# Shared expert's products between the first expert blocks, and two orders mended, in a two-layer mixture-of-experts kernel

## The chip, the cores and the metric

The kernel runs on one core of a Trainium2 chip as one program of some 58,000 instructions. Its engines work side by side, each in its own order, and wait for one another through semaphores: TensorE (PE; its loading of weights is shown as PEld), VectorE (DVE), ScalarE (ACT), GpSimd (POOL) and SyncE (SP), which issues most DMAs. The metric is the time in microseconds (us) that the core takes for the whole program. Before the change it is 2652.32 us, the median of 3 runs (2647.43 to 2654.61).

## The reference, cut to what matters

Two layers of a diffusion backbone with 256 latent and 256 context tokens, D = 1024. Each layer is a mixer (layer 0: mLSTM and SSD heads, layer 1: latent attention and RWKV-7 heads) and then a mixture of experts. In layer 0 the experts see all 512 tokens, in layer 1 the 256 latent ones. All of it is float32.

```
def swiglu(x, wg, wu, wd):
    return (silu(x @ wg) * (x @ wu)) @ wd            # 1024 -> 512 -> 1024

def moe(v, router_w, router_bias, w_gate, w_up, w_down, s_gate, s_up, s_down):
    aff = sigmoid(xt @ router_w)                      # 16 experts in 4 groups
    ...                                               # the best group, in it the two best experts
    out = swiglu(xt, s_gate, s_up, s_down)            # the shared expert: every token
    for e in range(16):
        out = out + gates[:, e:e + 1] * swiglu(xt, w_gate[e], w_up[e], w_down[e])
```

The routed experts are computed only for the tokens that chose them. Which ones these are is known on the chip alone, once the router has run.

## The kernel before, in words

**An expert layer** is the function `moe_block`. TensorE computes the router's logits and turns the 512 (or 256) tokens from columns to rows; DVE finds for each token its two experts (`route_masks`), and, once TensorE has counted the tokens of each expert ahead of each token (`positions`), a row number in a list sorted by expert (`route_slots`). GpSimd writes each token's row twice into the list `x_sorted` in HBM (`rows_scattered`). The list is cut into blocks of 32 rows; each expert fills whole blocks, at least one. There are 47 blocks in layer 0 and 31 in layer 1 (`n_blocks`); those that the tokens leave over at the end count to the last expert. For each block, TensorE multiplies its 32 rows by the gate and up weights of its expert in two halves (`gate_up`, lines 1569 and 1570), turns the hidden values (`turn_hidden`, line 1578) and multiplies by the down weights (`down`, line 1591); for each pair of blocks the rows of x are turned first (`turn_x`, line 1554).

**Weights.** An expert has 2 MB of gate, 2 MB of up and 2 MB of down weights, 6 MB in all. There is room for three experts, three places: place 0 and 1 in the arena, place 2 in the ring that elsewhere holds the streamed weights of other products, and in which the shared expert's three pieces lie when the layer starts. The blocks are dealt to the places in contiguous parts: place p takes the blocks from `first_of[p]` on, and step i of the loop takes the next block of place `i % 3`. So in layer 0 place 0 has the blocks 0 to 15, place 1 16 to 31, place 2 32 to 46; in layer 1 0 to 10, 11 to 20, 21 to 30. A block's weights are loaded only if its expert differs from that of the block before it (`cond=new`; a table on the chip tells), and always for the first block of a place. SP issues these loads in the order of the steps, the first half of gate and up (lines 1440 and 1441) after the place's last block is done with its first half, the second half after its second, the down weights (line 1444) one step later. A load that is not wanted is issued too, but moves nothing.

**The shared expert** is computed between the router and the first block, in one go: 4 gate products and 4 up products of 8 matmuls each (`shared_rows`), then the down products of 4 matmuls each (8 in layer 0, 4 in layer 1; line 368 as all products through the helper `mms`). Only when they are done can the ring be loaded as place 2. The tokens' rows for the first blocks are read into `m_x`, which lies over the shared expert's input, and so not before its gate and up products are over.

**The mixer of layer 0** has the function `project_rest`: 32 products, of which ACT splits each weight into a high part (line 680), POOL makes the low part (line 690), TensorE multiplies and ACT reads out the result (lines 944 to 948). Meanwhile DVE makes the gates' running sums; ACT's exponentials for it (lines 936, 793, 795) stand ahead of the products' first split, in the order in which ACT works.

## Time and profile before

| what | value |
|---|---|
| median of 3 runs | 2652.32 us |
| the profiled execution's own time | 2651.06 us |
| its span, first to last instruction | 2649.3 us |
| PE busy, share of the span | 81% |
| DVE, ACT, POOL busy | 38%, 27%, 13% |
| router and shared expert of layer 0, from 853 us to the first block at 959.86 | 107 us |
| blocks of layer 0 | to 1321 us |
| router and shared expert of layer 1, from 2268 us to the first block at about 2324 | 56 us |
| blocks of layer 1 | to 2617 us |

The positions are those of the profiled execution, in us from its first instruction. A group of the profile is a line of the kernel with its operation and its tiles (what it writes, an arrow, what it reads). A busy TensorE is not one at its peak. A time in brackets behind a row is idle time of the engine before that instruction, and what ended it. "PEclk" is the clock granted to TensorE, 1.00 being 2.4 GHz and 0.50 being 1.2 GHz. "SPq" and "ACTq" are the issues of DMAs by these engines.

### The profile page before, as it was taken

What the parts mean: (1) busy time and instruction counts of PE and PEld (TensorE: products, weight loads), DVE (VectorE), ACT (ScalarE), POOL (GpSimd) and SP (SyncE); (2) the same over time, 40 slices, a digit from 0 to 9 for tenths busy, and PEclk for the clock granted to TensorE, in tenths of its full rate; (3) what the DMA queues carried; (4) which work ended last, traced back from release to release, by engine and by line L of the source; (5) the groups of instructions that cost most, each with busy time, mean ns of one, the idle gap of its engine ahead of it and who ended that gap; (6) DMA issues with size and microseconds to landing.
All of it is one profiled execution on the core that took longest, in us unless ns stands there. A gap on an engine that the chain in (4) does not pass through costs nothing. (4 is left out here: it accounts for less than half of the span.)

```text
span 2649.3 us, 57779 instructions
## 1 busy us (share of the span) xinstructions
PE 2141.1 (81%) x25731; PEld 1417.6 (54%) x25731; DVE 1010.6 (38%) x1602; ACT 706.4 (27%) x1499; POOL 350.6 (13%) x232
## 2 busy tenths in 40 slices
PE   5879999788796987797838869867887888877776
PEld 2457764343483544454523458557887866633333
DVE  0352506756504211111142257556576652311112
ACT  2222622255413000010020232354644420100001
POOL 0223320000142100000010024222131100000000
PEclk7989998778897999998968889979999988888788
DMA  7244540320324478987731012000000023599994
GB/s 246 98 169 155 187 162 1 116 75 0 96 95 167 185 255 308 316 276 266 275 140 69 0 56 88 0 3 4 4 4 4 4 74 119 174 376 341 344 337 162
DMA packets 180957, 381.00 MB, mean 144 GB/s; under 512 B 11242, under 2 KB 40518, under 8 KB 180454
## 3 DMA queue, kind: packets, MB, share of 16 engines
q1 hardware_dynamic: 163118, 344.02, 36.5%
q10 hardware_dynamic: 14136, 20.72, 2.6%
q0 software_dynamic: 3456, 12.58, 1.3%
q8 instruction: 202, 3.31, 0.5%
q14 instruction: 45, 0.37, 0.0%
HBM read 634.46 MB, written 25.95 MB: 249 GB/s over the span
## 5 line engine op out<-in xcount | busy, mean ns | idle before, releaser
L1569 PE MATMUL banks<-arena 128*32 128x256 f32 x1696 | 238.4, 430 | 105.6 <-DMA arena<-in_exp_w_up_dram 105.6
L368 PE MATMUL banks<-parts 128*128 128x512 f32 (+1 forms) x1096 | 241.0, 373 | 23.6 <-DVE parts L382 20.4
L1570 PE MATMUL banks<-arena 128*32 128x256 f32 x1696 | 238.4, 430 | 0.0
L368 PEld LDWEIGHTS banks<-parts 128*128 128x128 f32 x1096 | 194.3, 192 | 59.7 <-DVE parts L382 11.5
L1569 PEld LDWEIGHTS banks<-arena 128*32 128x32 f32 x1696 | 107.1, 121 | 196.8 <-DMA arena<-in_exp_w_up_dram 114.2
L376 DVE TENSOR_TENSOR arena<-banks,arena 64x256 f32<-64x256 f32 (+3 forms) x128 | 65.2, 511 | 334.0 <-ACT arena L1633 264.4
L2225 PE MATMUL banks<-arena 64*64 64x64 f32 x4224 | 155.7, 221 | 45.1 <-DVE arena L379 18.1
L1633 ACT ACTIVATE arena<-banks 64x256 f32<-64x256 f32 x78 | 29.7, 380 | 588.5 <-PE banks L1570 588.5
L368 PE MATMUL banks<-arena,ring 128*128 128x256 f32 (+2 forms) x544 | 161.7, 460 | 12.7 <-PEq L315 12.7
L2225 PEld LDWEIGHTS banks<-arena 64*64 64x64 f32 x4224 | 144.0, 136 | 51.0 <-DVE arena L379 19.4
L2225 PE MATMUL banks<-ring 64*64 64x64 f32 x4224 | 156.0, 220 | 11.8 <-issue 11.6
L368 PE MATMUL banks<-arena 128*64 128x128 f32 (+9 forms) x492 | 135.8, 430 | 36.8 <-PEq L315 25.0
L2225 PEld LDWEIGHTS banks<-ring 64*64 64x64 f32 x4224 | 143.3, 135 | 12.7 <-issue 12.2
L368 PE MATMUL banks<-h_parts,parts_z 128*128 128x512 f32 x416 | 133.9, 402 | 17.2 <-POOL parts_z L690 13.3
L368 PEld LDWEIGHTS banks<-arena,ring 128*128 128x128 f32 (+1 forms) x544 | 105.4, 195 | 67.1 <-issue 56.0
L368 PEld LDWEIGHTS banks<-arena 128*128 128x128 f32 (+5 forms) x492 | 74.3, 196 | 89.5 <-issue 60.5
L1591 PE MATMUL banks<-arena 128*32 128x256 f32 x1696 | 107.0, 395 | 17.0 <-DMA arena<-in_exp_w_down_dram 17.0
L1784 POOL DMA_INDIRECT arena<-y_sorted,slot_ids x12 | 11.3, 945 | 746.1 <-DMA y_sorted<-arena 743.1
L1569 PE MATMUL banks<-ring,arena 128*32 128x256 f32 x800 | 99.9, 393 | 8.9 <-DMA ring<-in_exp_w_up_dram 8.9
L1570 PEld LDWEIGHTS banks<-arena 128*32 128x32 f32 x1696 | 106.6, 121 | 0.0
L690 POOL TENSOR_TENSOR parts_z<-ring,parts_z 128x1024 fp32r<-128x1024 f32 x34 | 84.3, 2482 | 158.4 <-ACT parts_z L680 139.1
L1229 PE MATMUL banks<-arena 128*64 128x256 f32 (+3 forms) x288 | 89.8, 467 | 13.8 <-DVE arena L1262 13.8
(341 smaller groups left out, 3772.8 us busy)
## 6 DMA issues: line engine op xcount, KB each, us to landing
arena<-in_exp_w_gate_dram SPq DMA_DIRECT2D x106, 1024.0 KB
arena<-in_exp_w_up_dram SPq DMA_DIRECT2D x106, 1024.0 KB
arena<-in_exp_w_down_dram SPq DMA_DIRECT2D x53, 2048.0 KB
ring<-in_exp_w_gate_dram SPq DMA_DIRECT2D x50, 1024.0 KB
ring<-in_exp_w_up_dram SPq DMA_DIRECT2D x50, 1024.0 KB
ring<-in_exp_w_down_dram SPq DMA_DIRECT2D x25, 2048.0 KB
ring<-in_w_mod_dram SPq DMA_DIRECT2D x24, 2048.0 KB, 8.0
ring<-in_ab_w_in_dram SPq DMA_DIRECT2D x10, 2048.0 KB, 12.8
```

The source lines that it names most:

```text
L368: m = nc.tensor.matmul(o, a, b, start=first and n == 0, stop=last and n == len(pairs) - 1)
L376: return nc.vector.tensor_tensor(o, a, b, ALU.mult)
L690: nc.gpsimd.tensor_tensor(low, landed_part(j), whole(high), ALU.subtract).then_inc(pool_done, pool.tick(("w low", j), *((let_go(key),) if ...
L1229: m = nc.tensor.matmul(o[:, c0:c1], a_xt[:, s, hd * SSP:(hd + 1) * SSP], weights_of[it % 3][:, s, c0:c1], start=d == 0 and k == 0, stop=d ...
L1569: nc.tensor.matmul(o[r:r + BLOCK, 0:256], x, up[:, k, c], start=k == 0, stop=k == KD - 1)
L1570: m = nc.tensor.matmul(o[64 + r:64 + r + BLOCK, 0:256], x, gate[:, k, c], start=k == 0, stop=k == KD - 1)
L1591: m = nc.tensor.matmul(ps[3 + i % 2][BLOCK * q:BLOCK * q + BLOCK, 0:256], x, w[:, k, 256 * q:256 * q + 256], start=k == 0, stop=k == 3)
L1633: nc.scalar.activation(m_sil[0:64, :], ps[i % 2][64:P, 0:256], ACT.Silu).then_inc(act_done, act.tick(("silu", i)))
L1784: nc.gpsimd.indirect_dma_start(m_yg[:, t, a, :], None, y_sorted, bass.IndirectOffsetOnAxis(ap=slots[:, t, a:a + 1], axis=0)).then_inc(y_ga ...
L2225: m = nc.tensor.matmul(view(d, n_)[half(d, hf, n_), p, :], now[d][a][rows, p, :], now[d][b][rows, p, :], start=q == 0, stop=q == len(pairs ...
```

## The change

It has three parts.

**1. In both expert layers** the shared expert's products are cut up. Two gate and two up products stay ahead of the first block; the other four and all down products (`fillers`, 12 in layer 0, 8 in layer 1) follow one block each. While they last, the blocks are dealt to the places 0 and 1 alone (`place`), and the third place is opened with the step after the last of them: its gate and up weights are issued ahead of those of step 5, its down weights once the last shared product is done. After that the order of the places is 2, 0, 1. The blocks 0 to 17, 18 to 34 and 35 to 46 now belong to the places 0, 1 and 2 in layer 0, and 0 to 11, 12 to 22 and 23 to 30 in layer 1. The rows of x, the shared hidden values and the blocks' outputs move to the room of `h` and `scratch`; so h is written to HBM (2 MB) before the first expert's weights are loaded, and read back behind the last ones. The shared products use the banks 5 and 6 in turn.

**2. In layer 1** DVE does `route_masks` ahead of its copies of the turned tokens, and `positions` follows the first gate product in both layers (before, the second one in layer 0, and the fifth product in layer 1).

**3. In `project_rest`** ACT's two exponentials that wait for the running maxima, and the two that the step sizes need, move from ahead of the first product to ahead of the fifth.

```
             def act_():
                 soft_act(tmp, "lf")
                 nc.scalar.activation(a_bias[:, 4:5], a_bias[:, 3:4], ACT.Exp).then_inc(act_done, act.tick("A"))
-                for e in range(2):
-                    act.wait_ge(*at(("m", e)))
-                    nc.scalar.activation(a_em[:, e], a_em[:, e], ACT.Exp, scale=-1.0).then_inc(act_done, act.tick())
-                soft_act(tmp32, "dt")
...
                 for j, (key, f) in enumerate(jobs):
+                    if j == 4:
+                        for e in range(2):
+                            act.wait_ge(*at(("m", e)))
+                            nc.scalar.activation(a_em[:, e], a_em[:, e], ACT.Exp, scale=-1.0).then_inc(act_done, act.tick())
+                        soft_act(tmp32, "dt")
...
-            in_place = [len(range(p, nb, 3)) for p in range(3)]
+            inside = True
+            fillers = [("g", 2), ("u", 2), ("g", 3), ("u", 3)] + [("d", d) for d in range(2 * nt)] if inside else []
+            place = [i % 2 for i in range(len(fillers))]
+            place += [(2, 0, 1)[j % 3] if inside else j % 3 for j in range(nb - len(place))]
+            in_place = [place.count(p) for p in range(3)]
             first_of = [sum(in_place[:p]) for p in range(3)]
+            nth = [place[:i].count(place[i]) for i in range(nb)]
+            ahead = [max((j for j in range(i) if place[j] == place[i]), default=None) for i in range(nb)]
+            opening = [place.index(p) for p in range(3)]
...
             def block_of(i):
-                return first_of[i % 3] + i // 3
+                return first_of[place[i]] + nth[i]
...
+                if inside:
+                    nc.sync.dma_start(h_saved, h[:]).then_inc(h_saved_done, 16)
                 load_half(0, 0, None)
                 load_half(0, 1, None)
                 load_down(0, None)
                 sp.wait_ge(*at("block table"))
...
+                for i in range(nb):
+                    if i == 5 and inside:
+                        open_third("halves")
+                    if i in opening:
+                        if i > 2:
+                            finish_down()
+                            open_third("down")
+                        continue
...
-                    sp.wait_ge(*at(("first half", i - 3)))
+                    sp.wait_ge(*at(("first half", ahead[i])))
                     load_half(i, 0, expert, cond=new)
-                    sp.wait_ge(*at(("gate up", i - 3)))
+                    sp.wait_ge(*at(("gate up", ahead[i])))
                     load_half(i, 1, expert, cond=new)
...
+                if inside:
+                    sp.wait_ge(*at(("x turned", ng - 1)))
+                    sp.wait_ge(*at(("shared d", 2 * nt - 1)))
+                    load(nc.sync, h[:], h_saved)
                 if issued[0] < len(pieces):
-                    sp.wait_ge(*at(("down", max(range(2, nb, 3)))))
+                    sp.wait_ge(*at(("down", max(j for j in range(nb) if place[j] == 2))))
                     stream_weights(issued[0] - 1)
...
+                if inside:
+                    tokens_away()
+                    shared_rows("g", 0)
+                    positions()
+                    shared_rows("u", 0)
+                    shared_rows("g", 1)
+                    shared_rows("u", 1)
+                    turn_x(0)
...
                     if i > 0:
                         down(i - 1)
+                    if i < len(fillers):
+                        kind, f = fillers[i]
+                        if kind == "d":
+                            shared_down(f)
+                        else:
+                            shared_rows(kind, f)
...
+                if l == 1:
+                    route_masks()
                 for j in range(1, 2 * nt, 2):
                     dve.wait_ge(*at(("tokens", j)))
                     nc.vector.tensor_copy(m_vtok[:, j // 2, 512:1024], ps[1 + j % 5]).then_inc(dve_done, dve.tick(("tokens out", j)))
-                route_masks()
+                if l == 0:
+                    route_masks()
...
+                if inside:
+                    dve.wait_ge(loads_landed, loads[0] + 16)
```

ACT in `project_rest`, before (line 933 is the last exponential that waits for nothing new, 936 the two that wait for the maxima, 793 and 795 those of the step sizes, 680 a split, 944 a read-out):

```order
L933 ACTIVATE arena<-arena 32x1
L936 ACTIVATE arena<-arena 8x512 x2
L793 ACTIVATE arena<-arena 32x512
L795 ACT_TABLE_LOAD
L795 ACTIVATE arena<-arena 32x512
L680 ACTIVATE parts_z<-ring 128x1024
L944 ACTIVATE arena<-banks 128x512
```

and after (line 954 is the former 936, 940 the former 944):

```order
L933 ACTIVATE arena<-arena 32x1
L680 ACTIVATE parts_z<-ring 128x1024
L940 ACTIVATE arena<-banks 128x512
L680 ACTIVATE parts_z<-ring 128x1024
L940 ACTIVATE arena<-banks 128x512
L490 ACTIVATE scratch<-banks 128x512
L680 ACTIVATE parts_z<-ring 128x1024
L940 ACTIVATE arena<-banks 128x512
L680 ACTIVATE parts_z<-ring 128x1024
L940 ACTIVATE arena<-banks 128x512
L954 ACTIVATE arena<-arena 8x512 x2
L793 ACTIVATE arena<-arena 32x512
```

Four splits and four read-outs now stand ahead of the exponentials.

TensorE in layer 0, from the last of the router's counts to the first block, before:

```order
L368 MATMUL banks<-arena,ones 128x16 x7
L368 MATMUL banks<-arena,ring 128x512 x48
L368 MATMUL banks<-ring,arena 128x512 x28
L1554 MATMUL banks<-ident,arena 128x64 x8
L368 MATMUL banks<-ring,arena 128x512 x4
L1569 MATMUL banks<-arena 32x256
```

and after (1629 is the former 1554, the turning of x; 1644 the former 1569, the first of a block's matmuls):

```order
L368 MATMUL banks<-arena,ones 128x16 x7
L368 MATMUL banks<-arena,ring 128x512 x24
L1629 MATMUL banks<-ident,h 128x64 x8
L1644 MATMUL banks<-arena 32x256
```

24 matmuls of the shared expert are left there where 80 stood; the others follow the blocks.

SP in layer 0, its issues after the block table has been read, before (lines 1440 and 1441 are a half of gate and up, 1444 is down; arena is place 0 or 1, ring is place 2):

```order
L1440 DMA arena<-in_exp_w_gate_dram 128x4x512
L1441 DMA arena<-in_exp_w_up_dram 128x4x512
L1440 ISA
L1440 DMA ring<-in_exp_w_gate_dram 128x4x512
L1441 DMA ring<-in_exp_w_up_dram 128x4x512
L1440 ISA
L1440 DMA ring<-in_exp_w_gate_dram 128x4x512
L1441 DMA ring<-in_exp_w_up_dram 128x4x512
L1444 DMA arena<-in_exp_w_down_dram 128x4x1024
L1444 DMA ring<-in_exp_w_down_dram 128x4x1024
```

and after, from the end of step 4's loads on (1460, 1461 and 1464 are the former 1440, 1441 and 1444):

```order
L1461 DMA arena<-in_exp_w_up_dram 128x4x512
L1464 DMA arena<-in_exp_w_down_dram 128x4x1024
L1452 TENSOR_LOAD arena
L1452 ISA x2
L1460 ISA
L1460 DMA ring<-in_exp_w_gate_dram 128x4x512
L1461 DMA ring<-in_exp_w_up_dram 128x4x512
L1460 ISA
L1460 DMA ring<-in_exp_w_gate_dram 128x4x512
L1461 DMA ring<-in_exp_w_up_dram 128x4x512
L1452 TENSOR_LOAD arena
L1452 ISA x2
```

The third place's gate and up loads have moved from behind step 1's to between step 4's and step 5's.

## Rows read from the trace of the kernel before

**Rows 1.** The page: span.
```profile
span 2649.3 us, 57779 instructions
```
**Rows 2.** Stages: PE, PEld, DVE, ACT, POOL busy (x), PEclk, DMA share, GB/s.
```profile
960.00:1321.00 361.00, 302.29 (x4790) 168.42 (x4784) 53.40 (x141) 31.61 (x70) 0.00 (x0) 0.92 0.83 294
2324.00:2617.00 293.00, 218.02 (x3158) 117.36 (x3154) 35.27 (x93) 20.75 (x46) 0.00 (x0) 0.85 0.95 334
```
**Rows 3.** TensorE's waits in the blocks of layer 0: us, times, longest.
```profile
PE banks L1569 <- DMA arena<-in_exp_w_up_dram: 46.3, 16, 6.7
PE banks L1591 <- DMA arena<-in_exp_w_down_dram: 5.4, 4, 1.5
PE banks L1569 <- DMA ring<-in_exp_w_up_dram: 5.4, 1, 5.4
PE banks L1591 <- DMA ring<-in_exp_w_down_dram: 1.5, 1, 1.5
```
**Rows 4.** The same in the blocks of layer 1.
```profile
PE banks L1569 <- DMA arena<-in_exp_w_up_dram: 59.2, 16, 6.3
PE banks L1591 <- DMA arena<-in_exp_w_down_dram: 11.5, 6, 2.7
PE banks L1569 <- DMA ring<-in_exp_w_up_dram: 3.4, 1, 3.4
PE banks L1591 <- DMA ring<-in_exp_w_down_dram: 0.7, 1, 0.7
```
**Rows 5.** Timeline of `project_rest`, TensorE and ACT: start us, us, instruction, idle before.
```profile
188.14 0.80 PE L368 MATMUL banks<-h_parts,parts_z 128*128 128x512 f32 x1 [13.29 <-POOL parts_z L690]
179.05 0.63 ACT L936 ACTIVATE arena<-arena 8x512 f32<-8x512 f32 x1 [13.00 <-DVE arena L841]
```
**Rows 6.** Timeline of TensorE in layer 0: shared products, and the first block.
```profile
888.99 41.45 PE L368 MATMUL banks<-arena,ring 128*128 128x512 f32 x96
931.38 24.27 PE L368 MATMUL banks<-ring,arena 128*128 128x512 f32 x56 [0.95 <-DVE arena L376]
...
959.86 0.40 PE L1569 MATMUL banks<-arena 128*32 128x256 f32 x1
```
**Rows 7.** Timeline of TensorE in layer 0: two down products, two blocks apart.
```profile
1133.12 1.93 PE L1591 MATMUL banks<-arena 128*32 128x256 f32 x32
...
1145.06 1.93 PE L1591 MATMUL banks<-arena 128*32 128x256 f32 x32
```
**Rows 8.** Issues of SP in layer 0: one made, one left out, the last made.
```profile
897.72 0.40 SPq L1440 DMA_DIRECT2D arena<-in_exp_w_gate_dram  x1
995.06 0.08 SPq L1440 DMA_DIRECT2D arena<-in_exp_w_gate_dram  x1
1296.63 0.38 SPq L1440 DMA_DIRECT2D arena<-in_exp_w_gate_dram  x1
```
**Rows 9.** The same in layer 1: the first after the table, the last made.
```profile
2306.06 0.39 SPq L1440 DMA_DIRECT2D arena<-in_exp_w_gate_dram  x1
2592.86 0.38 SPq L1440 DMA_DIRECT2D arena<-in_exp_w_gate_dram  x1
```
**Rows 10.** DMA from 2306 to 2560 us: total, SP's and ACT's queue.
```profile
DMA packets 38904, 88.90 MB, mean 350 GB/s; under 512 B 1630, under 2 KB 4325, under 8 KB 38879
...
q1 hardware_dynamic: 34403, 80.93, 90.0%
q10 hardware_dynamic: 4219, 6.69, 8.7%
```
**Rows 11.** Timelines: DVE starts the slots in both layers; ACT loads x.
```profile
889.26 0.41 DVE L1685 TENSOR_TENSOR arena<-banks,arena 128x240 f32<-128x240 f32 x1 [10.48 <-PE banks L368]
...
2298.11 0.28 DVE L1685 TENSOR_TENSOR arena<-banks,arena 128x112 f32<-128x112 f32 x1 [14.07 <-PE banks L368]
...
2310.96 1.73 ACTq L1607 DMA_DIRECT2D arena<-x_sorted  x4
```
**Rows 12.** Layer 0 after a wait of 6.7 us: PE busy, PEclk, DMA share, GB/s.
```profile
983.00:986.50 3.50, 3.50 (x33) 0.50 1.06 406
```

More of the change, by code:

```diff
@@ L1449, in sp_, with open_third, finish_down @@
                 sp.wait_ge(*at("block table"))
-                second, third = number_at(block_of(1)), number_at(block_of(2))
-                load_half(1, 0, second)
-                load_half(1, 1, second)
-                for k in range(2):
-                    sp.wait_ge(*at(("let go", piece_at[("sh", l, k)])))
-                load_half(2, 0, third)
-                load_half(2, 1, third)
-                sp.wait_ge(*at(("let go", piece_at[("sh", l, 2)])))
-                load_down(1, second)
-                load_down(2, third)
-                for i in range(3, nb):
+                second = number_at(block_of(opening[1]))
+                load_half(opening[1], 0, second)
+                load_half(opening[1], 1, second)
+                def open_third(which):
+                    third = number_at(block_of(opening[2]))
+                    if which == "halves":
+                        for k in range(2):
+                            let_go_of_shared(k)
+                        load_half(opening[2], 0, third)
+                        load_half(opening[2], 1, third)
+                    else:
+                        let_go_of_shared(2)
+                        load_down(opening[2], third)
+                if inside:
+                    load_down(opening[1], second)
+                else:
+                    open_third("halves")
+                    let_go_of_shared(2)
+                    load_down(opening[1], second)
+                    open_third("down")
+                waiting = []
+                def finish_down():
+                    for b, expert, new in waiting:
+                        sp.wait_ge(*at(("down", ahead[b])))
+                        load_down(b, expert, cond=new)
+                    waiting.clear()
+                for i in range(nb):
+                    if i == 5 and inside:
+                        open_third("halves")
+                    if i in opening:
+                        if i > 2:
+                            finish_down()
+                            open_third("down")
+                        continue
                     b = block_of(i)
@@ L1489, in pe_, with shared_rows, shared_down @@
                     m.then_inc(pe_done, pe.tick(("tokens", j)))
[L1491 removed]
+                def shared_rows(kind, f):
+                    key = "gu".index(kind)
                     w = weights(("sh", l, key))
[L1493 to L1511 removed]
+                    if inside and f:
+                        pe.wait_ge(*at((("shared silu", "shared hidden")[key], f - 1)))
+                    mms(shared_bank(kind, f)[:, 0:n], [(w[:, k, f * P:(f + 1) * P], m_v[:, k, c0:T]) for k in range(KD)]).then_inc(
+                        pe_done, pe.tick((kind, f), *((let_go(("sh", l, key)),) if f == 3 else ())))
+                def shared_down(d):
                     t, half = divmod(d, 2)
+                    w = weights(("sh", l, 2))
                     if d == 0:
@@ L1638, in act_ @@
                             load_x(g + 2)
+                    if i < len(fillers) and fillers[i][0] == "g":
+                        shared_silu(fillers[i][1])
                 for t in range(nt):
```

133 lines of the change are left out of this document (77 added, 56 removed).

## The prediction
> **What bounds the kernel now.** I read the page first, then the busy times by stage, since 81% of busy TensorE is an average over stages with different limits; then TensorE's waits in each stage, and at last the timelines: of TensorE for what a product and a block take, of SP for which loads move data. The span is 2649.3 us [rows 1], the execution's own time 2651.06 (1.8 more), the median of the three runs 2652.32. In the blocks of layer 0 the DMA engines are busy 83% of 361 us, in those of layer 1 95% of 293 us [rows 2]: both want weights faster than they come. TensorE waits there for nothing but weights, 46.3 + 5.4 + 5.4 + 1.5 = 58.6 us in layer 0 [rows 3] and 59.2 + 11.5 + 3.4 + 0.7 = 74.8 us in layer 1 [rows 4]. A third, single wait stands in the mixer of layer 0: TensorE idles 13.29 us for a low part that POOL can't make, because ACT stands 13.00 us in front of an exponential for DVE's running maxima [rows 5].
>
> A block without a wait takes 5.97 us of TensorE (two in 1145.06 - 1133.12 = 11.94) [rows 7]. So layer 0 should need 959.86 [rows 6] + 47 x 5.97 + 58.6 = 1299; it needs 1321 [rows 2]. The other 22 us are the end of the chain and the clock: after a wait of 6.7 us the granted clock is 0.50, the level of 1.2 GHz, and the matmuls take twice as long [rows 12]. That is 0.38 us for each us waited. Layer 1: 2324 + 31 x 5.97 + 74.8 = 2584 against 2617 [rows 2], 0.44 for each.
>
> **ACT's order in `project_rest`: -15 us.** Now four splits and read-outs stand ahead of the exponentials. ACT can split as soon as TensorE is through with a room, so the 13.29 us [rows 5] go, and with them the slow clock behind them: after the wait of [rows 12] 3.5 us ran at half speed, so I count 1.7 us. The exponentials then wait for nothing (the maxima were ready at 179.05), and what they take (2 x 0.63 [rows 5], as much again for the step sizes, and the change of tables, an estimated 4 us in all) lies beside the fifth product, which is already split. DVE's chain of step sizes starts some 6 us later; its next customer is the sixteenth product, far behind. If that cover fails, at most 5 us come back: -10 to -15, and I take -15, as the wait has one cause. Stages behind it move along unchanged; weights in the ring come earlier too, since their slots are let go earlier.
>
> **How many experts are loaded: one more in each layer.** A load that moves data shows 0.37 us or more at its first issue, one left out 0.07 to 0.09 [rows 8]. Read through all steps, layer 0 loads at the steps 3, 5, 9, 10, 14, 15, 19, 24, 28, 30, 36, 37, 42 and 46 (14; the last is in [rows 8]), which with the three openings is 17 experts. Step i holds block i // 3 of its place, so experts begin at the blocks 1, 3, 5, 8, 10, 12, 14, 19, 22, 25, 28, 31, 33 and 36. Sixteen experts have 15 beginnings behind block 0, so one of 16 and 32, where places begin, is the fifteenth. The new places begin at 18 and 35. Neither is a beginning, so both repeat an expert that another place holds: 15 + 3 = 18 loads. In layer 1 the moving steps are 4, 6, 7, 10, 12, 13, 16, 18, 19, 21, 24, 25 and 30 (13; the last in [rows 9]), 16 with the openings, so both 11 and 21 are beginnings; the new places begin at 12 (a beginning: block 12 is step 4 now) and 23 (none): 14 + 3 = 17. The place that is opened last in layer 1 thus holds nothing but the last expert once more. An expert is 6.29 MB; SP's queue moved 80.93 MB in 254 us where the engines were never idle [rows 10], so it costs 19.7 us of a full queue.
>
> The Trainium skill (DMA: Bandwidth & Descriptors, Where 436 GB/s comes from) puts what one core gets from HBM at about 358 GB/s, by which an expert would cost an estimated 17.6 us and the sum would end 2 us lower. The trace's 350 GB/s with everything counted [rows 10] agrees nearly; the rule speaks against the change too, which adds bytes where the limit is bytes.
>
> **Layer 1: +11 us.** It is the queue that decides here. It starts to run full with the first load behind the table, at 2306.06 [rows 9], 7.95 us after DVE begins with the slots [rows 11]. The counts now follow one product instead of five; a product of 256 tokens takes half of one of 512, which is 41.45 / 6 = 6.9 [rows 6], so 4 x 3.45 = 13.8 us go. DVE's masks ahead of the copies keep the tokens 3 us longer and the clock falls for a moment: 4 us come back. The stream starts 9.8 us earlier and is 19.7 longer: +9.9; I add 1 for the opening, in which only two places take loads. From below: the extra load falls into the 5% of 293 us in which the queue rests [rows 2], -5. From above: the third place's halves, 4.2 MB or 12 us, stand ahead of step 5's in the queue and wholly in TensorE's way, +23.
>
> **Layer 0: +7 us, and +2 behind it.** The first block starts earlier. The slots begin one product less a short wait earlier, 889.26 - 5.9 = 883.3 [rows 11]. In layer 1 ACT issues the rows of x 12.9 us after the slots begin [rows 11]; with twice the scatters beside a full queue I take 22, some 12 for landing, turning and reading out, so 917 to 920: 919. Then the blocks, 280.6, and the shared products between them: 4 x 6.9 + 8 x 24.27 / 7 = 55.4 [rows 6]. Without waits that is 1255. The waits: before, the moving steps form five close pairs and four lone ones. A lone load has three steps, 17.9 us, for two halves that take 13 of the full queue; I put it at 1.5 us, which leaves (58.6 - 6) / 5 = 10.5 for a pair. Now they fall on 2, 3, 6, 9, 10, 15, 17, 19, 25, 26, 31, 35, 37, 41 and 43. Steps 2 and 3 are hidden by products of 6.9 us each: 0. Step 6 stands behind the third place's halves: 8. 9 and 10 have short products between: 7. Down of the third place, not issued before the last shared product: 2. 15, 17, 19: 12. The pair 25, 26: 10. 31: 1.5. The looser pairs 35, 37 and 41, 43: 6 each. Together 53, with 20 for clock and end: 1328 against 1321. Ends: 35 us of waits, -17; 65 and a start at 923, +20. Behind the blocks h is read back (2 MB) and the next layer's weights are issued one step later, both beside the gathering of y: +2, from 0 to 5. Saving h costs nothing: 2 MB ahead of a load that has over 40 us until the first block.
>
> The Trainium skill (DMA: Bandwidth & Descriptors, Issuing engines are not separate DMA queues) has the loads that ACT issues share the 16 engines with SP's. Here ACT's queue takes 8.7% beside SP's 90.0% [rows 10], so the rows of x for the first block, alone in the queue before, now arrive beside a whole expert; without it the start would be some 5 us earlier, and the sum the same, as weights decide.
>
> **The sum.** 2651.06 - 15 + 11 + 7 + 2 = 2656; the runs' median stands 1.3 higher, which I leave out. Some 0.3% (8 us) is what a measurement can tell from no change. All low ends together give 2614, all high ends 2691.
>
> **The rivals.** *A, the two sides cancel:* 2656, own range 2646 to 2668. *B, the overlap works:* the 55 us of products in a stage that lacks weights halve the waits of layer 0, to 35, and in layer 1 the extra load falls into idle time. For it: 83%, not 100%, of the DMA engines in layer 0. Against: the waits come from loads that bunch, and the new deal bunches those of places 0 and 1 into the first 12 (8) steps. 2651 - 15 - 17 - 3 + 2 = 2618. The Trainium skill (TensorE: Matmul & The Clock Gate, Loop structure matters more than you think) wants matmuls back to back with transfers behind them; this is what B would make of it. *C, slower, starved by two places:* while the shared products last, each load has one step's time less, and the third place's halves are issued ahead of step 5's although they are wanted four to seven steps later. If their 12 us are paid in full in both layers, instead of 8 and 1: 2656 + 4 + 11 = 2671, with clock 2676. It decides if TensorE's wait at step 5 or 6 exceeds about 12 us. *D, the order of ACT moves the wait instead of removing it:* the fifth product waits for ACT's detour and DVE's delay reaches the sixteenth: 2656 + 12 = 2668. Against it: DVE's work there is done long before.
>
> **Chances.** A 0.46, B 0.24, C 0.22, D 0.08. A's range reaches past 2660, so of its chance 0.28 falls within 0.3%, 0.04 below, 0.14 above; B gives 0.23 faster, 0.01 none; C and D give 0.06 within and 0.24 slower. Faster 0.27, same 0.35, slower 0.38. The range takes in C, D and B's upper half: 2630 to 2680.
>
> **What would show it.** In `project_rest` no wait of TensorE over 2 us before the fifth product. In layer 0 the first block at 915 to 923 and the last before 1335 less 15; 18 and 17 loads that move data; in layer 1 a DMA share of 0.9 or more and the longest waits at the steps 5 and 9. I am wrong if waits for weights fall under 45 us in layer 0 (B) or exceed 70 (C), or if layer 1's blocks end earlier, counted from its start.

## The result: 2680 us, 1.1% slower, and the profile after

The changed kernel takes 2680.16 us (median of 7 runs, 2667.32 to 2687.83) against 2652.32 us of the kernel before (7 runs beside it): ratio 1.011, 95% interval 1.009 to 1.014. 2656 was predicted, from 2630 to 2680. The profiled execution took 2685.76 us, 5.6 above the median, so differences between the two spans come out larger than the 27.8 us between the medians.

The DMA total of the kernel before, and then the span, which answers to [rows 1], and the DMA total of the kernel after:

```profile
DMA packets 180957, 381.00 MB, mean 144 GB/s; under 512 B 11242, under 2 KB 40518, under 8 KB 180454
```
```profile
span 2684.0 us, 57784 instructions
...
DMA packets 186814, 401.97 MB, mean 150 GB/s; under 512 B 11467, under 2 KB 40743, under 8 KB 185799
```

20.97 MB more are two experts (2 x 6.29) and h out and back in both layers (4 x 2.10). The stages of the kernel after, which answer to [rows 2]: each layer from its start to its first block, and its blocks. The columns are those of [rows 2].

```profile
843.20:907.30 64.10, 51.36 (x200) 35.37 (x201) 16.33 (x52) 6.96 (x10) 7.80 (x8) 0.79 0.80 285
907.30:1329.50 422.20, 367.56 (x4918) 192.96 (x4918) 59.65 (x150) 32.81 (x72) 0.00 (x0) 0.92 0.79 276
2282.40:2329.00 46.60, 29.80 (x131) 26.12 (x132) 12.76 (x50) 5.30 (x8) 3.93 (x4) 0.68 0.93 329
2329.00:2648.60 319.60, 244.35 (x3254) 132.13 (x3254) 38.22 (x98) 21.52 (x48) 0.00 (x0) 0.86 0.92 332
```

A layer starts here with ACT's loading of the table for the router's sigmoid (852.9 and 2268.2 before, 843.2 and 2282.4 after). From there to the last down product layer 0 takes 64.1 + 422.2 = 486.3 us, before 1321.3 - 852.9 = 468.4: +17.9. Layer 1 takes 366.2 against 349.1: +17.1. From `project_rest` to the mLSTM it is 205.5 against 220.4: -14.9. Behind layer 0's blocks it is 952.9 against 946.9 to the start of layer 1, +6.0, and the tail has 35.4 against 32.0, +3.4; the stages ahead have +3.4 and +1.8. That is all of the 34.7 us between the spans.

TensorE's waits of the kernel after (us, times, longest), in the blocks of layer 0 and of layer 1, which answer to [rows 3, 4]:

```profile
PE banks L1644 <- DMA arena<-in_exp_w_up_dram: 45.5, 13, 6.7
PE banks L1644 <- DMA ring<-in_exp_w_up_dram: 4.4, 1, 4.4
PE banks L1667 <- DMA arena<-in_exp_w_down_dram: 4.3, 3, 3.6
...
PE banks L1644 <- DMA arena<-in_exp_w_up_dram: 62.7, 15, 11.5
PE banks L1667 <- DMA arena<-in_exp_w_down_dram: 10.7, 4, 3.6
```

The waits for weights in layer 0 are 54.2 us, where before they were 58.6: 59 us of shared products between the blocks have brought a net 4. In layer 1 they are 73.4 us against 74.8. And there is a wait that the kernel before does not have. TensorE's timeline at the first block of layer 0 and of layer 1 (the bracket is the idle time ahead of a row and what ended it):

```profile
905.31 1.12 PE L1629 MATMUL banks<-ident,h 64*128 64x64 f32 x8 [10.88 <-DMA h<-x_sorted]
907.27 0.61 PE L1644 MATMUL banks<-arena 128*32 128x256 f32 x1 [0.84 <-ACT arena L1699]
...
2327.04 1.11 PE L1629 MATMUL banks<-ident,h 64*128 64x64 f32 x8 [11.95 <-DMA h<-x_sorted]
```

It waits 10.9 and 12.0 us for the rows of x. Then the granted clock is 0.50, the level of 1.2 GHz, and the first block's gate and up products take 6.1 us in layer 0 instead of 3.7. TensorE in layer 0 behind the wait, and behind that stretch (last three numbers: PEclk, DMA share, GB/s):

```profile
905.30:912.00 6.70, 5.84 (x56) 3.46 (x60) 0.00 (x0) 0.60 (x1) 0.00 (x0) 0.50 0.93 285
912.40:915.00 2.60, 2.60 (x31) 1.48 (x24) 0.42 (x1) 0.98 (x2) 0.00 (x0) 1.00 0.97 283
```

### The profile page after: what moved, and what is told of

It is laid out like the page before. It is cut to its first block and busy times, and to the rows that moved or that the text cites. A ratio compares the mean times of both kernels' runs of the same rounds, so it can differ in the third digit from the quotient of the medians.

```text
span 2684.0 us, 57784 instructions
## 1 busy us (share of the span) xinstructions
PE 2163.7 (81%) x25731; PEld 1423.8 (53%) x25731; DVE 1018.2 (38%) x1602; ACT 706.7 (26%) x1499; POOL 351.2 (13%) x232
## 3 DMA queue, kind: packets, MB, share of 16 engines
q0 software_dynamic: 3456, 12.58, 1.3%
## 5 line engine op out<-in xcount | busy, mean ns | idle before, releaser
L1644 PE MATMUL banks<-arena 128*32 128x256 f32 x1856 | 255.9, 424 | 110.0 <-DMA arena<-in_exp_w_up_dram 108.2
L1645 PE MATMUL banks<-arena 128*32 128x256 f32 x1856 | 255.9, 424 | 0.0
L1644 PEld LDWEIGHTS banks<-arena 128*32 128x32 f32 x1856 | 115.2, 120 | 214.8 <-DMA arena<-in_exp_w_up_dram 117.4
L368 PEld LDWEIGHTS banks<-parts 128*128 128x128 f32 x1096 | 194.7, 192 | 59.9 <-DVE parts L382 11.5
L1715 ACT ACTIVATE arena<-banks 64x256 f32<-64x256 f32 x78 | 29.7, 381 | 646.3 <-PE banks L1645 646.3
L2324 PE MATMUL banks<-arena 64*64 64x64 f32 x4224 | 156.0, 222 | 46.1 <-DVE arena L379 17.9
L376 DVE TENSOR_TENSOR arena<-banks,arena 64x256 f32<-64x256 f32 (+2 forms) x120 | 60.9, 508 | 310.4 <-ACT arena L1715 275.3
L1667 PE MATMUL banks<-arena 128*32 128x256 f32 x1856 | 122.3, 408 | 17.2 <-DMA arena<-in_exp_w_down_dram 15.0
L1645 PEld LDWEIGHTS banks<-arena 128*32 128x32 f32 x1856 | 114.6, 120 | 0.0
L1831 DVE COPY arena<-banks 128x128 f32<-128x128 f32 x78 | 22.7, 291 | 201.4 <-PE banks L1654 201.4
```

What stands on the lines that cost most here:

```text
L368: m = nc.tensor.matmul(o, a, b, start=first and n == 0, stop=last and n == len(pairs) - 1)
L376: return nc.vector.tensor_tensor(o, a, b, ALU.mult)
L1644: nc.tensor.matmul(o[r:r + BLOCK, 0:256], x, up[:, k, c], start=k == 0, stop=k == KD - 1)
L1645: m = nc.tensor.matmul(o[64 + r:64 + r + BLOCK, 0:256], x, gate[:, k, c], start=k == 0, stop=k == KD - 1)
L1667: m = nc.tensor.matmul(ps[3 + i % 2][BLOCK * q:BLOCK * q + BLOCK, 0:256], x, w[:, k, 256 * q:256 * q + 256], start=k == 0, stop=k == 3)
L1715: nc.scalar.activation(sil[0:64, :], ps[i % 2][64:P, 0:256], ACT.Silu).then_inc(act_done, act.tick(("silu", i)))
```

## The experiments

All ratios are against the kernel before on the same chip (medians 2648.7 to 2652.3). The theories by number: **1**, a repeated expert lengthens a full queue; **3**, the late start, the wait for x and the clock behind it; **5**, the time from the release of a place to its next use makes the waits; **6**, a load that is free to go stands behind another one's wait in SP's queue. Theory 2 and two rivals are named in the expectations.

| kernel | median us | ratio (95%) | layer 0 | layer 1 |
|---|---|---|---|---|
| before | | 1 | 468.4 | 349.1 |
| after | 2680.2 | 1.011 (1.009-1.014) | 486.3 | 366.2 |
| e1_act | 2634.6 | 0.994 (0.992-0.996) | 469.2 | 349.3 |
| e2_orders | 2627.0 | 0.9905 (0.988-0.993) | 468.1 | 339.5 |
| e3_layer0 | 2653.7 | 1.001 (0.999-1.003) | 486.6 | 341.5 |
| e4_layer1 | 2657.8 | 1.003 (1.001-1.005) | 467.1 | 369.7 |
| e5_norepeat | 2677.3 | 1.0105 (1.008-1.013) | 479.3 | 374.9 |
| e6_third_later | 2678.8 | 1.011 (1.009-1.013) | 486.8 | 368.8 |
| e8_deal_alone | 2684.3 | 1.013 (1.0105-1.015) | 500.4 | 354.3 |
| e9_orders_norepeat | 2638.7 | 0.996 (0.994-0.997) | 475.0 | 342.4 |
| e10_skip_l1 | 2672.3 | 1.008 (1.0055-1.010) | 487.1 | 356.2 |
| e11_fill_x | 2668.0 | 1.006 (1.004-1.009) | 473.9 | 362.8 |
| e12_skip_l0 | 2665.5 | 1.005 (1.0035-1.006) | 477.4 | other routing |
| e14_no_save_l1 | 2683.1 | 1.013 (1.011-1.015) | 483.5 | 368.7 |
| e15_down_behind | 2675.8 | 1.010 (1.008-1.013) | 486.5 | 361.4 |
| e16_both_behind | 2673.5 | 1.0095 (1.007-1.012) | 483.1 | 363.1 |
| e17_filled_behind | 2676.7 | 1.010 (1.007-1.013) | 480.5 | 366.2 |

The last two columns are one trace each, from the layer's start to its last down product. Where layer 0 or 1 is the code of the kernel after, it repeats within 4 us (486.3, 486.6, 487.1, 483.5; 366.2, 369.7). So a difference of 4 us between two single traces is not a finding.

Three kernels leave out work to see what it costs, and their output is not the reference's: e10_skip_l1 and e12_skip_l0 leave out loads, e14_no_save_l1 a store.

**ACT's order alone** (e1_act: the kernel before with part 3 of the change alone).

> The kernel before with ACT's new order in project_rest alone; both expert layers as before. The trace after has the stage from project_rest to the mLSTM 14.9 us shorter (205.5 against 220.4). If that gain is ACT's order's alone and the stages behind it move along, this kernel takes 2652 - 15 = 2637 us (ratio 0.994) and the expert layers take what they took: 468 and 349 us from their start to their last down product. If instead the gain is given back later (weights in the ring don't come earlier, so the next stage waits), it takes 2645 or more and a later stage is longer than before.

0.994: the whole gain stays.

**The orders alone** (e2_orders).

```
-            inside = True
+            inside = False
```

> The kernel after, with its flag for the shared products between the blocks set to false in both layers: the shared expert runs ahead of the blocks, the experts are dealt in turn to three places, h stays where it is. What is left of the change is ACT's order in project_rest, the masks ahead of the token copies in layer 1 and TensorE's counting product behind the second shared product. If the masks' order is a gain by itself, it is the first kernel less 0 to 5 us: 2632 to 2637. If it costs (tokens read out later, the shared products behind them), 2637 to 2642. All theories of the expert layers say that the loss of the kernel after is gone here: under 2645.

0.9905, 8 us better than ACT's order alone and below what was expected: the best kernel of all. The gain lies in layer 1, 339.5 against 349.3; two other kernels with this order and no products between layer 1's blocks have 341.5 and 342.4. SP's timeline there has its first load behind the block table 26.6 us after the layer's start; in the kernel before it is 37.8:

```profile
2286.06 0.39 SPq L1460 DMA_DIRECT2D arena<-in_exp_w_gate_dram  x1
```

From there to the last down product the DMA engines are busy 95% of the time, and the layer ends earlier by nearly as much as the queue starts earlier (9.8 of 11.2 us).

**One layer at a time** (e3_layer0, e4_layer1: `inside = l == 0` and `inside = l == 1`, and the count that ACT waits for at the store of h to match).

> The kernel after with the shared products between the blocks in layer 0 alone; layer 1 runs its shared expert ahead of the blocks. The traces have layer 0 longer by 17.9 us to its last down product and by 6.0 behind it. If the layers are independent, this is the kernel of orders alone + 24: about 2659 to 2661. If the repeated expert is what costs (18 loads against 17), at most 19.7 us of it are the queue's and the rest is h's way out and back. If the loss in layer 1 was caused by layer 0 (the ring's weights issued 15 us later), this one is near the kernel after, 2675 or more.

> The kernel after with the shared products between the blocks in layer 1 alone. The traces have layer 1 longer by 17.1 us to its last down product, and the tail by 3.4. Independent layers give the kernel of orders alone + 20: about 2655 to 2657, and with the one of layer 0 alone the differences add up to that of the kernel after (some 44). In the trace the step 5 and the step 9 should have the longest waits again, 11.5 and 10.0 us, whatever layer 0 does.

Against the orders alone layer 0 costs 26.7 us of the medians and layer 1 30.8; together 57.5, the kernel after 53.2. That is a sum within the intervals: no sign that one layer's loss causes the other's. With the orders as the base layer 1 costs more than the two first traces showed, since the masks' gain had hidden some of it.

**The deal alone** (e8_deal_alone: `inside` false, but `place` as in the kernel after; no shared product follows a block, and the third place is loaded ahead of the blocks, as in the kernel before).

```
-            place += [(2, 0, 1)[j % 3] if inside else j % 3 for j in range(nb - len(place))]
+            place += [(2, 0, 1)[j % 3] for j in range(nb - len(place))]
```

> The kernel of orders alone (shared expert ahead of the blocks, h where it is) with the deal of the kernel after: the first 12 steps of layer 0 and 8 of layer 1 to two places in turn, 18 and 17 experts loaded. It tells the deal from the products between the blocks. Orders alone took 2627; both together 2680. If the deal alone is the loss (theory 1 and the bunching of two places' loads), it has all of it: layer 1 from 339.5 to about 362, layer 0 from 468 to 480 or more, since without the products between them the blocks of two places come faster still: 2662 or more. If the loss is made by the shared products between the blocks (start, clock, h), this kernel is under 2650.

It is as slow as the kernel after, with the shared expert ahead of the blocks, no wait for x and h untouched: 32 us more than the orders alone in layer 0, 15 in layer 1. TensorE's waits in the blocks of layer 0, of this kernel and of the orders alone:

```profile
PE banks L1645 <- DMA arena<-in_exp_w_up_dram: 67.5, 18, 11.6
PE banks L1668 <- DMA arena<-in_exp_w_down_dram: 4.8, 3, 2.4
PE banks L1645 <- DMA ring<-in_exp_w_up_dram: 3.3, 1, 3.3
```
```profile
PE banks L1644 <- DMA arena<-in_exp_w_up_dram: 39.6, 14, 6.4
PE banks L1644 <- DMA ring<-in_exp_w_up_dram: 8.5, 3, 6.4
PE banks L1667 <- DMA arena<-in_exp_w_down_dram: 4.4, 3, 1.6
PE banks L1667 <- DMA ring<-in_exp_w_down_dram: 1.5, 1, 1.5
```

75.6 us against 54.0. So the products between the blocks do cover waits in layer 0, 75.6 to 54.2, and the layer is 14.1 us shorter with them; but they only cover as much as the deal to two places makes. In layer 1 the waits go from 79.1 to 73.4, and the layer is longer with them, 366.2 against 354.3. Part of the loss is at the start: 59 and 31 us of products have moved behind the first block, which comes only 42.8 us earlier in layer 0 (64.1 against 106.9 us after the layer's start) and 8.8 in layer 1 (46.6 against 55.4). Of the 16 and 23 us between, 11 and 12 are TensorE's wait for the rows of x.

**The repeated experts** (e5_norepeat, e10_skip_l1, e12_skip_l0, e9_orders_norepeat).

```
+            for i in ((45,), (25, 28))[l]:      # e5
+                place[i] = (0, 2)[l]
...
+                    b = nb - 1 if l == 1 and i == 25 else b      # e10; e12: l == 0 and i in (41, 43)
                     new = nc.sync.value_load(m_table[0:1, 48 + b:49 + b], min_val=0, max_val=1)
...
+            if l == 0:      # e9, on the orders alone
+                place[46] = 2
```

> The kernel after with three steps dealt to another place: in layer 0 step 45 to the first place (19, 17 and 11 blocks instead of 18, 17 and 12), in layer 1 the steps 25 and 28 to the third (12, 9 and 10 instead of 12, 11 and 8). All places then begin where an expert begins and each layer loads 16 experts instead of 18 and 17: 3 x 6.3 MB less. Theory 1 (a repeated expert lengthens a full queue by 19.7 us): in layer 1, 19.7 of its 17.1 us more come back, start to last down product falls from 366 to about 347; in layer 0, where the queue is only 79% busy, 5 to 15 of two experts: 2680 - 20 - 10 = 2650. Theory 2 (the opening with two places and the late start cost, the bytes don't matter): layer 1 stays above 360 and the sum above 2672.

Layer 0 gave 7.0 us; layer 1 became 8.7 us longer with one expert less. The new deal puts the steps 25 and 26 into one place, and 28 and 29 too. SP takes the steps in order: before it comes to step 30's load it waits for step 29's place, which step 28 holds. TensorE then waits 7.2 us for step 30's gate and up weights; in the kernel after it didn't. The run doesn't tell the theories apart, so the load was left out without moving anything:

> The kernel after without one load: in layer 1 step 25 (second place, the last expert, which the third place holds too) computes with the weights that lie in its place already, so its part of the output is that of another expert; order, waits and places are unchanged. The kernel with another deal did two steps in a row in one place, and SP's queue stood behind the second of them; here nothing is moved. Theory 1 (bytes: a repeated expert costs 19.7 us of a full queue): layer 1 falls from 366.2 to about 347, the kernel from 2680 to 2661. Theory 5 (it is the time from the release of a place to its next use that makes a wait, and step 25 is a lone load with three steps, which has no wait in the trace): layer 1 falls by 0 to 6 us, by what the steps 27 and 30 no longer wait: 2674 to 2680.

356.2, 10.0 us less: between the two. The waits of step 27 (7.6 us) are gone and 1.8 come back at step 30; the DMA share of the blocks falls from 0.92 to 0.90.

> The kernel after without two loads in layer 0: the steps 41 and 43 (experts that another place holds too) compute with the weights in their places, so layer 0's output is another one and layer 1's routing with it; only layer 0's own time, from its start to its last down product, is read. It was 486.3 us with 18 loads. Theory 1 in the form that bytes decide: 19.7 to 39 us less. Theory 5: step 43's wait of 7.4 us goes, with the clock behind it 3 us, and step 41, without a wait, gives nothing: 475 to 479, still longer than the 468 of the kernel of orders alone with 17 loads.

477.4, as theory 5 had it: 8.9 less, of which 7.4 is the wait of step 43.

> The kernel of orders alone with step 46 of layer 0 dealt to the third place instead of the second: 16, 15 and 16 blocks instead of 16, 16 and 15, so that all places begin with an expert's first block and 16 experts are loaded instead of 17. In the kernel before the load of step 46 is the last of the layer, with waits right ahead of the end. If a repeated expert costs where the queue is not full (83% in layer 0), layer 0 falls from 468 by 3 to 10 us: 2617 to 2624, the best of all. If the queue's idle shares hide it, 2625 to 2629.

A miss: one expert less and 12 us more (ratio 0.996 against 0.9905), 7 of them in layer 0. By the new starts the loads of layer 0 fall on the steps 8, 9 and 10 one behind the other, where they fell on 5, 9 and 10. TensorE waits 17.9 us at these three instead of 16.5 at the former, and 13.2 at 15, 17 and 19 instead of 9.8 at 14, 15 and 19. Where loads fall weighs as much as how many there are.

**The third place's halves** (e6_third_later: `i == opening[2] - 2` for `i == 5`).

> The kernel after with the third place's halves issued two steps ahead of its first block (ahead of step 10's loads in layer 0, of step 6's in layer 1) instead of ahead of step 5's. In layer 1 TensorE waited 11.5 us at step 5, the rival that 4.2 MB (12 us) stand in the way there. If the queue is full anyway, the wait only moves to steps 6 to 9 and the sum stays within 4 us of 2680. If it was paid for nothing (the halves wanted three steps later than loaded), the wait at step 5 falls under 3 us and layer 1 ends 5 to 10 us earlier: 2670 to 2675. In layer 0 step 6 loses its 6.4 us of wait, and step 9 or 10 has them or not.

Step 5's wait falls from 13.4 to 5.4 us, and down of step 5 waits 7.1 instead: 368.8 against 366.2. In layer 0 the 6.4 us of step 6 become 10.4 at step 10. The wait only moves.

**Products in front of the first block** (e11_fill_x: the third gate and up product in layer 0, the third and fourth in layer 1 go ahead of `turn_x(0)`; places unchanged).

```
                     shared_rows("u", 1)
+                    for f in range(2, 2 + early):      # early: 1 in layer 0, 2 in layer 1
+                        shared_rows("g", f)
+                        shared_rows("u", f)
                     turn_x(0)
```

> The kernel after with shared products put in front of the first block, where TensorE waits 10.9 and 11.9 us for the rows of x: the third gate and up product in layer 0 (14 us), the third and fourth in layer 1 (14 us). The places and the deal stay the same. If these waits are a loss of their own (theory 3), both layers become shorter by them and by the half clock of the first block, 10 to 14 us each: 2680 - 24 = 2656. If the blocks' weights decide all the same (theory 5: the steps 2 to 6 lack the products now, and wait for their weights instead), what is gained ahead of the first block comes back as waits at the steps 2 and 3 in layer 0 and 2 to 5 in layer 1: 2673 to 2682.

Each theory is right in one layer. Layer 0 gains 12.4 us in this trace: the first block starts 2.4 later and runs at a granted clock of 1.00 (its gate and up products take 3.7 us, not 6.1), 5.2 of waits appear at step 2, and 14 us of products no longer stand behind it. Layer 1 gains 3.4, no more than single traces differ: its waits for weights go from 73.4 to 81.0. TensorE's waits in its blocks:

```profile
PE banks L1650 <- DMA arena<-in_exp_w_up_dram: 73.6, 19, 11.5
PE banks L1673 <- DMA arena<-in_exp_w_down_dram: 7.4, 4, 2.2
```

**The store of h** (e14_no_save_l1: no store in layer 1).

> The kernel after without the store of h at the start of layer 1 (2.1 MB); what is read back behind the blocks is h as layer 0 left it in memory, so the sum behind layer 1 is another one. Layer 1 moved 121.4 MB against 111.3 MB in the kernel of orders alone, at 0.33 MB per us in both. If all bytes of a full queue count, the store's 2.1 MB are 6 us of layer 1's 366.2: 360, the kernel at 2674. If the store is hidden (8.4 MB of it and the first expert take 25 us, and the next load waits for the table until 28.4 us after the layer's start), layer 1 stays within 2 us of 366 and the wait for the rows of x at 11.9.

Hidden: 368.7 us, and 11.6 of wait for the rows of x.

**SP's queue** (e15_down_behind, e16_both_behind, e17_filled_behind). SP's timeline in layer 1 of the kernel after, around the opening of the third place:

```profile
2409.44 10.84 SPq L1464 DMA_DIRECT2D arena<-in_exp_w_down_dram  x2
2433.02 0.37 SPq L1464 DMA_DIRECT2D ring<-in_exp_w_down_dram  x1
2434.85 0.37 SPq L1460 DMA_DIRECT2D arena<-in_exp_w_gate_dram  x1
```

From 2420.3 to 2433.0 it issues nothing: the third place's down weights wait for the last shared product, and step 9's load, free since 2415, stands behind. TensorE pays at step 9:

```profile
2449.35 0.64 PE L1644 MATMUL banks<-arena 128*32 128x256 f32 x1 [10.02 <-DMA arena<-in_exp_w_up_dram]
```

The DMA engines between 120 and 160 us after the layer's start, of the kernel after, of the deal alone, and of e15_down_behind (last two numbers: DMA share, GB/s):

```profile
2402.40:2422.40 20.00, 17.83 (x159) 8.33 (x153) 2.66 (x6) 1.36 (x3) 0.00 (x0) 0.79 0.86 313
2422.40:2442.40 20.00, 16.93 (x215) 8.32 (x213) 3.65 (x8) 1.36 (x3) 0.00 (x0) 0.98 0.70 253
```
```profile
2415.60:2435.60 20.00, 12.22 (x172) 6.60 (x172) 2.12 (x6) 0.98 (x2) 0.00 (x0) 0.84 1.03 364
2435.60:2455.60 20.00, 14.48 (x208) 7.61 (x212) 2.26 (x6) 1.36 (x3) 0.00 (x0) 0.84 1.03 356
```
```profile
2394.80:2414.80 20.00, 17.66 (x157) 8.43 (x154) 2.66 (x6) 1.36 (x3) 0.00 (x0) 0.79 0.86 304
2414.80:2434.80 20.00, 18.76 (x249) 9.46 (x247) 3.94 (x9) 1.36 (x3) 0.00 (x0) 1.00 0.97 353
```

```
                         if i > 2:
                             finish_down()
-                            open_third("down")
                         continue
...
                     load_half(i, 0, expert, cond=new)
+                    if inside and i == opening[2] + 1:
+                        open_third("down")
```

> The kernel after with the third place's down weights issued behind the first halves of the step that follows its opening (step 9 in layer 1, step 13 in layer 0) instead of ahead of them. Theory 6 (SP's queue stands at the wait for the last shared product, and step 9's load behind it): in layer 1 step 9's load is issued some 12 us earlier, its wait of 10.0 us falls under 4, the hole in the queue goes, layer 1 falls from 366.2 to 354 to 358 and the kernel from 2680 to about 2670. In layer 0 no load moves at step 13, so nothing changes: 484 to 488. Rival (two places have no room for a load, whoever stands in front of it): the wait stays at 8 or more, the sum within 4 us of 2680.

Half of it at most. The second of the two stretches fills up, layer 1 takes 361.4 us in this trace instead of 366.2 and 369.7, but the second halves of step 9 still stand behind SP's wait: step 9's wait moves from its first half to its second and is 8.8 us. The first hole stays. By the medians the gain is not shown: 1.010 against 1.011, with intervals that overlap.

> The kernel of the run before, and the third place's halves issued right ahead of step 7's loads in layer 1 and of step 11's in layer 0 instead of ahead of step 5's. With theory 6 step 5's wait of 11.5 us falls under 3 without moving to step 9, whose load now isn't behind a wait: layer 1 at 348 to 354, 2664. If the queue is full from step 5 on, the wait moves to the steps 7 to 10 as it did before, and this kernel is within 3 us of the one before.

363.1: the wait moves from step 5 to step 7, by the rival. The stretch from 120 to 140 us is full here (share 1.03) and the next one has the hole (0.77).

> The kernel with shared products in front of the first block (2668) with the third place's down weights issued as in the first run of this call. If the two repairs are independent, layer 0 takes 474 and layer 1 362.8 less 9 to 12 us: 2657 to 2660, slower still than the kernel of orders alone, 2627, by the repeated experts (about 19) and h's way back. If they share one cause, 2664 or more.

Over 2664: the two repairs do not add up. Layer 1 takes 366.2 us, no less than the kernel after, with 9.8 us of wait at step 9. Layer 0 took 480.5 where the same code up to step 13 took 473.9, which I can't explain; so the gain of the products in front of the first block is 12.4 us in one trace and 5.8 in another.

## Why the prediction was wrong

The sum put the kernel 5 us above the profiled execution of the kernel before; between the two spans it is 34.7. Of the 29.7 missing, layer 0 has 10.9, layer 1 6.1, the stretches behind the two layers 4.0 and 3.4, and 5.2 lie in stages ahead of layer 0 that the change does not touch. Two terms failed: the 1 us for the opening in layer 1 and the 20 us for clock and end in layer 0.

**ACT's order, -15:** right. -14.9 by the stages, 0.994 alone; behind its first product there TensorE has no wait above 0.6 us, where [rows 5] had 13.29.

**The loads, 18 and 17:** right. The deal alone moves 393.58 MB, 12.58 more than before, two experts.

**Layer 1, +11, measured +17.1:** the start of the stream was right (28.2 us after the layer's start against 37.8, 9.6 earlier; 9.8 predicted). But the masks and counts alone give all of it: 9.6 us without any product between the blocks. The term for the rest, 19.7 + 1, was 26.7 (366.2 - 339.5), and is made of other things than I wrote. The repeated expert is worth 10.0, not 19.7, once taken away. "I add 1 for the opening, in which only two places take loads" is the step that failed: the opening and the products in it cost 16.7 us, not 1. That the term was only 6 us short is luck, since the expert was put 9.7 too high. The deal alone divides the 26.7: it makes the layer 14.8 us longer, 10.0 for the repeated expert and about 5 for the two places; the other 11.9 come only with the products between the blocks and the third place that is opened late for them. In those 11.9 lie the wait for x (3.4 or less by e11_fill_x) and SP's wait for the last shared product (4.8 by e15_down_behind, nothing by e17_filled_behind); some 4 us stay open. These shares are rough, as each is a difference of two traces.

A hole in the queue that no run with these products fills stands around the first block, between 40 and 60 us after the layer's start. The kernel after and the deal alone in layer 1 (last two numbers: DMA share, GB/s):

```profile
2322.40:2342.40 20.00, 14.52 (x166) 9.45 (x170) 0.71 (x2) 1.96 (x4) 0.00 (x0) 0.75 0.73 234
```
```profile
2335.60:2355.60 20.00, 19.34 (x120) 9.32 (x124) 3.61 (x6) 1.23 (x3) 0.00 (x0) 1.00 1.05 334
```

The kernels that load the third place ahead of the blocks have a load to issue there, the kernel after has none: its third buffer still holds the shared expert's weights. By 0.73 against 1.05 of 20 us that is an estimated 6 us of a full queue; what it cost at the layer's end was not measured. The marks in layer 1, a DMA share over 0.9 and the longest waits at the steps 5 and 9, came true (0.92; 11.5 and 10.0).

**Layer 0, +7, measured +17.9:** the first block came 64.1 us after the layer's start (66 predicted), the products between took 59.2 (55.4), the waits 55.5 with all causes (53). By steps: 6.4 at step 6 (8 predicted), 3.6 at 9 and 10 (7), 15.4 at 15, 17 and 19 (12), 9.8 at 25 and 26 (10), 1.6 at 31, 8.9 and 7.4 at the last pairs (6 each). What failed is "with 20 for clock and end": blocks times 5.97, products and waits leave 27 of 422.2 us, where the kernel before already had 22. TensorE is busy 98.4 us with the blocks' down products instead of 94.6, and 2.4 more with the first block at half clock. So the layer is 11 us longer than forecast: 7 for clock and end, 4 for the products, 2.5 for the waits, less 2 for the start. Small misses, all but the start in one direction. The mark that the last block ends before 1320 was missed (1329.5). The wait for x was in the forecast of the start, but not as something that could have been filled.

Two ends of the range were added wrongly. Layer 0's lower end, -17, counts from the kernel before, its upper end, +20, from the forecast; counted like the lower one it is about +27, and +17.9 lies inside. All high ends together give 2689 as they stand, not 2691. Nor is half of 58.6 the 35 that B takes.

**h, and behind the layers, +2 and 0:** measured +6.0 and +3.4 in this trace. Over ten kernels whose layer 0 has the products between its blocks (all but e12_skip_l0), layer 0's end to layer 1's start is 951.1 us on average (948.8 to 956.2), over the six others 948.2 (946.4 to 951.0): +3. The tails with and without average 33.9 and 32.4. So the size was about right, and the rest is this trace's.

**The rivals.** C gave 2676, nearest to the truth. Its first half, that with two places each load has less time, is borne out: the deal alone is as slow as the kernel after. Its second half, from which its number comes, is that the third place's halves stand ahead of step 5's. The mark for it, over 12 us at step 5, came true in layer 1 only with both halves of the step counted (11.5 + 1.9 = 13.4), and e6_third_later refutes it: with the halves moved the time stays. So C's number is near for a cause that is only in part the right one. B was half right: the products cover 21 us of waits in layer 0, as many as the deal makes. D is refuted: ACT's order alone gave 15 us, where D had 3. None of the signs of being wrong appeared (waits in layer 0 under 45 or over 70 us, layer 1's blocks ending earlier): what went wrong stood in terms that they did not watch.

**Summed up,** against the orders alone (2627.0) the kernel after loses 53 us: 18 in layer 0, 27 in layer 1, some 4 behind them, and 4 that I can't place and that are within what runs of one kernel differ. In layer 0 the deal alone loses 32 and the products between the blocks give 14 back; in layer 1 the deal loses 15 and the products another 12. Keeping the two orders and leaving the shared expert where it was is the version that beats both: 2627 us, 0.9905.

## What to carry to other kernels

Products moved between blocks are worth the waits that they cover less what the moving takes away from the transfers: here it took a third buffer, and the deal to two made 22 us of waits in layer 0, as many as the products covered. Ask of each such move which buffers the work that stays behind still holds. Where a queue is nearly full, look for what starts it: an order that had its first load 11 us earlier gave 10 us, while products put into a wait of 12 us gave 3. And in a queue that is served in order, read what a load waits for together with what waits behind it.

## What the runs showed that I had not expected

Where the queue was nearly full (DMA share 0.92 to 0.95), layer 1's blocks moved 332 to 337 GB/s over some 300 us, with products between them or without (before, the orders alone, the deal alone, after, e11_fill_x). Fewer bytes did not mean as much less time: two experts less gave 8.9 and 7.0 us in layer 0, one less 10.0 in layer 1, and in two kernels, where the loads' steps moved too, one less cost 7 and 9. A single wait of 10.9 us at the start of layer 0's blocks came with the 1.2 GHz level over the next 6.7 us, nearly the whole first block; with 14 us of products put into that wait the first block had a granted clock of 1.00.
